# Two up projections of an fp32 transformer block on one Trainium2 core: the high part of the weights times both parts of the activations in one 512-column matmul

## The reference

```python
h = rms_norm(x, ffn_norm_w[layer])
gu = h @ w_gate_up[layer]                      # (256, 1024) @ (1024, 5632)
x = x + (jax.nn.silu(gu[..., :FFN_DIM]) * gu[..., FFN_DIM:]) @ w_down[layer]     # FFN_DIM = 2816
```

## Time and profile before

| what | value |
|---|---|
| median of 3 runs | 1063.54 us (1063.42 to 1064.06) |
| the profiled execution: first to last instruction (span) | 1061.5 us |
| median less span | 2.0 us |
| PE busy | 1045.6 us, 99% |
| DVE busy | 744.9 us, 70% |
| ACT busy | 605.3 us, 57% |
| granted TensorE clock, mean | 1.000 |

### The profile page before, as it was taken

The page is one execution under the profiler, slowest core; times in us unless marked ns, Lnnn a source line. Parts: engine busy times, 40 slices in busy tenths (PEclk is TensorE's granted clock), DMA queues, the critical chain, the costliest instruction groups (busy, mean ns, idle before and its releaser), DMA issues.

```text
span 1061.5 us, 23965 instructions
## 1 busy us (share of the span) xinstructions
PE 1045.6 (99%) x8650; PEld 1009.8 (95%) x8650; DVE 744.9 (70%) x1250; ACT 605.3 (57%) x1100; POOL 152.8 (14%) x160
## 2 busy tenths in 40 slices
PE   8999999999999999999999998999999999999998
PEld 7989999999999889999999998999898999999998
DVE  6875876665555878966655558878867569998743
ACT  7654764445545677654455445665766657666532
POOL 3100021111110000211111110000101034454300
PEclk9999999999999999999999999999999999999999
DMA  8533465555665322555556664444233445555563
GB/s 298 180 134 99 135 227 180 192 179 173 180 188 176 129 100 78 199 196 191 180 178 184 178 194 140 148 151 140 95 126 120 140 159 187 187 179 179 177 199 100
DMA packets 52488, 174.45 MB, mean 164 GB/s; under 512 B 5952, under 2 KB 7232, under 8 KB 52288
## 3 DMA queue, kind: packets, MB, share of 16 engines
q1 hardware_dynamic: 52416, 173.46, 50.0%
HBM read 172.39 MB, written 1.05 MB: 163 GB/s over the span
## 4 chain that ended last, share of the span: by engine, by line
PE 86%; DVE 6%; ACT 3%; issue 1%; DMA 1%; ACTq 0%; SPq 0%; DVEq 0%
PE bank L744 15%; PE bank L745 15%; PE bank L746 15%; PE scores L744 9%; PE scores L745 9%; PE scores L746 9%; DVE ring_lo L1620 2%; PE bank L729 2%; PE bank L730 1%; PE bank L731 1%; PE scores L955 1%; DMA ring_raw<-w_up 1%; ACT ring_hi L1147 1%; DVE tmp L1757 1%; PE bank L873 1%
## 5 line engine op out<-in xcount | busy, mean ns | idle before, releaser
L1620 DVE TENSOR_TENSOR ring_lo<-ring_raw,ring_hi 128x1024 fp32r<-128x1024 f32 (+2 forms) x343 | 399.4, 1167 | 60.3 <-ACT ring_hi L1147 54.5
L1147 ACT ACTIVATE ring_hi<-ring_raw 128x1024 fp32r<-128x1024 f32 (+2 forms) x343 | 341.0, 997 | 71.3 <-PE scores L746 34.0
L744 PE MATMUL bank<-xw_hi,ring_hi 128*128 128x256 f32 x1048 | 302.4, 289 | 1.4 <-DVE ring_lo L1620 0.6
L745 PE MATMUL bank<-xw_lo,ring_hi 128*128 128x256 f32 x1048 | 296.3, 283 | 0.0
L746 PE MATMUL bank<-xw_hi,ring_lo 128*128 128x256 f32 x1048 | 296.2, 283 | 0.0
L744 PEld LDWEIGHTS bank<-xw_hi,ring_hi 128*128 128x128 f32 x1048 | 200.6, 191 | 7.5 <-issue 5.1
L745 PEld LDWEIGHTS bank<-xw_lo,ring_hi 128*128 128x128 f32 x1048 | 200.7, 192 | 0.1
L746 PEld LDWEIGHTS bank<-xw_hi,ring_lo 128*128 128x128 f32 x1048 | 200.6, 191 | 0.0
L744 PE MATMUL scores<-xw_hi,ring_hi 128*128 128x256 f32 x528 | 150.2, 284 | 0.5 <-DVE xw_lo L1626 0.5
L745 PE MATMUL scores<-xw_lo,ring_hi 128*128 128x256 f32 x528 | 149.4, 283 | 0.0
L746 PE MATMUL scores<-xw_hi,ring_lo 128*128 128x256 f32 x528 | 149.4, 283 | 0.0
(11 more groups left out here) (247 smaller groups left out, 1868.5 us busy)
## 6 DMA issues: line engine op xcount, KB each, us to landing
ring_raw<-w_up SPq DMA_DIRECT2D x132, 512.0 KB, 3.2
ring_raw<-w_in SPq DMA_DIRECT2D x85, 512.0 KB, 3.2
ring_raw<-w_down SPq DMA_DIRECT2D x48, 512.0 KB, 3.6
ring_raw<-w_down SPq DMA_DIRECT2D x24, 384.0 KB, 3.9
ring_raw<-w_oa SPq DMA_DIRECT2D x16, 256.0 KB, 2.6
ring_raw<-w_ob SPq DMA_DIRECT2D x16, 256.0 KB, 2.9
ring_raw<-w_oa SPq DMA_DIRECT2D x8, 512.0 KB, 3.2
ring_raw<-w_ob SPq DMA_DIRECT2D x8, 512.0 KB, 3.3
```

The source lines that it names most:

```text
L744: mm(bank[b][:, 0:T], w_hi, tile(hi, t), start=kk == 0, stop=False)
L745: mm(bank[b][:, 0:T], w_hi, tile(lo, t), start=False, stop=False)
L1147: A(ring_hi[:, slot * DM:slot * DM + width], ring_raw[:, slot * DM:slot * DM + width], ACT.Copy).then_inc(hi_done, 1)
L1620: V.tensor_tensor(ring_lo[:, a:b], ring_raw[:, a:b], ring_hi[:, a:b].bitcast(f32), SUB).then_inc(lo_done, 1)
```

## The change

In `up0` and `up1` alone (`HALVES`), high weights by both parts of the activations become one matmul of 512 columns: the low and high parts now lie in one buffer, and the moving operand is a pattern of two pieces of 256 columns. The high weights are loaded once instead of twice. Columns 0 to 255 of the bank then hold high by high plus low weights by high activations, columns 256 to 511 high weights by low activations. The two halves must be added. Since this is done by reading one half from SBUF, ACT first copies the second half of the bank to SBUF (`copy_low`), DVE adds the first half to it, and a second DVE instruction multiplies with `rstd`, in place. Two semaphores are new, `low_copied` and `halves_summed`. All other projections keep their three matmuls; for them only the names of the buffers change.

```diff
+HALVES = ("up0", "up1")
...
+        self.halves = name in HALVES
...
+        low_half = u[:, 0:2 * T]
...
+        def hi_and_lo(parts, a, width=T):
+
+            return parts[:, :].rearrange("p (n c) -> p n c", n=2)[:, :, a:a + width]
...
+            def products(ps, a, parts, t, start, stop, halves=False):
+
+
+                w_hi, w_lo = ring_hi[:, a:a + P], ring_lo[:, a:a + P]
+                x_parts = hi_and_lo(parts, t * T)
+                if halves:
+                    mm(ps[:, 0:2 * T], w_hi, x_parts, start=start, stop=False)
+                else:
+                    mm(ps[:, 0:T], w_hi, x_parts[:, 0, :], start=start, stop=False)
+                    mm(ps[:, 0:T], w_hi, x_parts[:, 1, :], start=False, stop=False)
+                return mm(ps[:, 0:T], w_lo, x_parts[:, 0, :], start=False, stop=stop)
...
-                    mm(bank[b][:, 0:T], w_hi, tile(hi, t), start=kk == 0, stop=False)
-                    mm(bank[b][:, 0:T], w_hi, tile(lo, t), start=False, stop=False)
-                    last = mm(bank[b][:, 0:T], w_lo, tile(hi, t), start=False, stop=end)
+                    last = products(bank[b], a, parts, t, kk == 0, end, ph.halves)
...
+            def copy_low(layer, ph, i, c):
+
+                n = 2 * FT * layer + 4 * i + c
+                act.wait_ge(tile_done, ph.tile(i, c)[1] + 1)
+                if not (type(n) is int and n < 2):
+                    act.wait_ge(halves_summed, n - 1)
+                A(two(low_half, c % 2), bank[ph.bank(i, c)][:, T:2 * T], ACT.Copy).then_inc(low_copied, 1)
+
             def swiglu(layer):
                 def after(ph, i, c):
                     h = c // 2
                     p = FT * layer + 2 * i + h
+                    copy_low(layer, ph, i, c)
                     if c % 2 == 0:
                         act.wait_ge(out_ready, ph.out(i, c) + 1)
                         silu_gate(p, h, two(gate, h))
...
-                    V.tensor_tensor(two(val if c % 2 else gate, h), ps, rstd[:, :], MUL).then_inc(out_ready, 1)
+                    dst = two(val if c % 2 else gate, h)
+                    n = 2 * FT * layer + 4 * i + c
+                    dve.wait_ge(low_copied, n + 1)
+                    V.tensor_tensor(dst, ps, two(low_half, c % 2), ADD).then_inc(halves_summed, 1)
+                    dve.wait_ge(halves_summed, n + 1)
+                    V.tensor_tensor(dst, dst, rstd[:, :], MUL).then_inc(out_ready, 1)
```

More of the change, by code:

```diff
@@ L343, in program @@
         ring_raw = sb("ring_raw", RING * DM)
[L344 to L349, removed]
+        ring_parts = sb("ring_parts", 2 * RING * DM, f32r)
+        act_parts = sb("act_parts", 2 * FT * T, f32r)
+        xw_parts = sb("xw_parts", 2 * KT * T, f32r)
+        ring_hi, ring_lo = ring_parts[:, 0:RING * DM], ring_parts[:, RING * DM:2 * RING * DM]
+        act_hi, act_lo = act_parts[:, 0:FT * T], act_parts[:, FT * T:2 * FT * T]
+        xw_hi, xw_lo = xw_parts[:, 0:KT * T], xw_parts[:, KT * T:2 * KT * T]
         x = sb("x", KT * T)
@@ L433, in program @@
         ffn_hi, ffn_lo = sem("ffn_hi"), sem("ffn_lo")
+        low_copied, halves_summed = sem("low_copied"), sem("halves_summed")
         np_sq, np_ms, np_ln, np_rt, np_nt, np_out = (sem(f"norm_{s}") for s in ("sq", "ms", "ln", "rt", "nt", "out"))
@@ L703, in _, with project @@
             mm = nc.tensor.matmul
-            def project(ph, i, c, hi, lo, ready, halfway=None):
+            def products(ps, a, parts, t, start, stop, halves=False):
[7 more added lines that the diff above has]
+                return mm(ps[:, 0:T], w_lo, x_parts[:, 0, :], start=False, stop=stop)
+            def project(ph, i, c, parts, ready, halfway=None):
                 slot, g = ph.tile(i, c)
@@ L727, in project @@
                             o = bank[b][:, tt * T:(tt + 1) * T]
[L728 to L731, removed]
+                            x_tok = hi_and_lo(parts, t * T + tt * P, P)
+                            mm(o, x_tok[:, 0, :], w_hi, start=not second and k == 0 and tt == 0, stop=False)
+                            mm(o, x_tok[:, 0, :], w_lo, start=False, stop=False)
+                            last = mm(o, x_tok[:, 1, :], w_hi, start=False, stop=second and k == 3 and tt == 1)
                     last.then_inc(tile_done, 1)
@@ L741, in project, with project_first_two @@
                     a = slot * DM + k * P
-                    w_hi, w_lo = ring_hi[:, a:a + P], ring_lo[:, a:a + P]
                     end = part == ph.per - 1 and k == ph.blocks[part] - 1
-                    mm(bank[b][:, 0:T], w_hi, tile(hi, t), start=kk == 0, stop=False)
-                    mm(bank[b][:, 0:T], w_hi, tile(lo, t), start=False, stop=False)
-                    last = mm(bank[b][:, 0:T], w_lo, tile(hi, t), start=False, stop=end)
+                    last = products(bank[b], a, parts, t, kk == 0, end, ph.halves)
                 last.then_inc(tile_done, 1)
-            def project_first_two(ph, hi, lo, ready):
+            def project_first_two(ph, parts, ready):
                 for part in range(2):
@@ L757, in project_first_two @@
                                 ready(t)
[L758 to L762, removed]
+                            last = products(b, c * DM + t * P, parts, t, t == 0, t == KT - 1)
                         if part:
@@ L777, in project_group @@
                             n = ph.out0 + m
-                            b = bank[ph.bank_of[n]][:, 0:T]
+                            b = bank[ph.bank_of[n]]
                             if k0 == 0:
@@ L784, in project_group @@
                                     pe.wait_ge(*mixed(layer, t))
[L785 to L789, removed]
+                                last = products(b, slot * DM + (j * ks + k) * P, act_parts, t, k == 0, k == ks - 1)
                             if k1 == ks:
@@ L813, in root_by_token, with run @@
                 issued["root"] += 1
-            def run(name, hi, lo, ready, q=None, then=None, halfway=None):
+            def run(name, parts, ready, q=None, then=None, halfway=None):
                 ph = PH[name]
                 if name == "kv":
-                    project_first_two(ph, hi, lo, ready)
+                    project_first_two(ph, parts, ready)
                 for c in range(ph.body):
                     if name != "kv" or c >= 2:
-                        project(ph, 0, c, hi, lo, ready, halfway)
+                        project(ph, 0, c, parts, ready, halfway)
                     if name[:2] in ("kv", "in") and c == (3 if name == "kv" else 2):
@@ L829, in run @@
                     for c in range(ph.body):
-                        project(ph, 1, c, hi, lo, ready)
+                        project(ph, 1, c, parts, ready)
                 elif ph.turns > 1:
@@ L833, in run @@
                         for c in range(ph.body):
-                            project(ph, i, c, hi, lo, ready)
+                            project(ph, i, c, parts, ready)
             def stream_ready(q):
@@ L1113, in _ @@
                 mm(bank[6][:, 0:T], tmp[:, 0:P], tmp[:, 0:T], start=True, stop=True)
-            run("kv", act_hi, act_lo, stream_ready(0), 0)
+            run("kv", act_parts, stream_ready(0), 0)
             for layer in range(3):
@@ L1117, in _ @@
                 n_in = PH[f"in{layer}"].n
-                run(f"in{layer}", xw_hi, xw_lo, stream_ready(q), q, follow(layer, 0), amid(layer, 0))
-                run(f"oa{layer}", act_hi, act_lo, mixed_ready(layer), None, follow(layer, n_in), amid(layer, n_in))
+                run(f"in{layer}", xw_parts, stream_ready(q), q, follow(layer, 0), amid(layer, 0))
+                run(f"oa{layer}", act_parts, mixed_ready(layer), None, follow(layer, n_in), amid(layer, n_in))
                 project_group(layer)
-                run(f"up{layer}", xw_hi, xw_lo, stream_ready(q + 1), q + 1)
-                run(f"down{layer}", act_hi, act_lo, ffn_ready(layer))
+                run(f"up{layer}", xw_parts, stream_ready(q + 1), q + 1)
+                run(f"down{layer}", act_parts, ffn_ready(layer))
         @block.scalar
```

## The result

The changed kernel takes 1113.62 us (1112.15 to 1114.25), beside 1063.8 us for the kernel before: a ratio of 1.0465, 95% interval 1.0452 to 1.0478, 49.8 us more. The profiled executions have spans of 1111.5 and 1061.5 us, 50.0 us apart. The forecast was 1118.5 us, within 1100 to 1145.

A forecast was written before the change was run, and what follows sets the result against it. The prediction took a closed ring of ACT and DVE waits, 7.03 us per pair against PE's 5.55, as bound: 27.5 us late per up phase, 55.0 on 1061.5, plus 2.0 outside the span, gives 1118.5 us (range 1100 to 1145).

The forecast's parts named there:

- the ring: Closed path of waits between ACT and DVE in the up0 and up1 loops: 7.03 us per pair; chance 0.82.
- PE's pair: PE's time for a gate and a value tile in the up phases: 5.55 us forecast, 5.76 before.
- hand-offs: Six gaps per pair from an instruction's end to the start of the one waiting for it: 0.53 us in all.
- the one from add to multiply: DVE's multiply waiting for its add, twice per pair: taken as 0.10 us, between rows of 0.04 and 0.15.
- DVE to silu: ACT's silu waiting for DVE's multiply, once per pair: 0.12 us.
- The lower bound: Every hand-off at 0.03 us and the loop as short as written-out code: pair 6.68 us, total 1104.5 us.
- The cover: Weight splits running ahead of PE at the start of an up phase, hiding the first pairs; used up at tile 6.
- tile 47: Tile in down0 whose split follows ACT's table load: forecast ready at 300.6 us, 27.5 us late.
- the table load: ACT's load after the last `ffn_split` of an up phase, before tile 47's split; lateness grows from 25.1 to 27.5 us.
- the forecast 13 ns: PE's gain per contraction block in up0 and up1 from merging two matmuls: 9.4 us over 704 blocks.
- the fall: Rival: stalls in each pair drop PE's clock to 1.2 GHz in the up phases, 1280 us if it stayed low; chance 0.05.
- The dear matmul: Rival: the 512-column matmul's two-piece operand streams at half pace in the up phases, 1206 us; chance 0.03.
- The third rival: PE stays the bound in the up phases and its 9.4 us gain shows: 1054 us; chance 0.08 faster, 0.02 within 0.2%.

The follow-up runs named there:

- order: Changed kernel with ACT's `ffn_split` of a pair moved one step later, behind the copy of the next gate tile: 1057.07 us, ratio 0.9931; once more, 1058.35 us.
- extra_beside: Changed kernel plus one 256-column DVE multiply per pair, behind the even step's split, where DVE stands idle: 1113.16 us, ratio 1.0459.
- extra_on_ring: Changed kernel plus one 256-column DVE multiply per pair, between the odd step's multiply and its split: 1128.48 us, ratio 1.0602.
- pe_only: Changed kernel without ACT's copy and DVE's add, one product left out of both up projections, 512-column matmul kept: 1057.21 us, ratio 0.9925.
- three_mm: Changed kernel with the 512-column matmul taken apart into two of 256 columns; copy, add and multiply kept: 1113.57 us, ratio 1.0456.
- ffn_later: Changed kernel with `ffn_split` moved past ACT's next split only, in front of the next gate tile's copy: 1072.07 us, ratio 1.0064.
- copy_first: Changed kernel with ACT's copy moved in front of the split of its step, `ffn_split` unmoved: 1059.37 us, ratio 0.9949; once more, 1057.95 us.

## Why the prediction was right

**The bound and the ring.** The step that decided, that the queues' fixed order closes a ring longer than PE's pair, was right: the changed kernel waits at each of the edges named, `order` cuts one of them and the loss is gone, and `extra_beside` and `extra_on_ring` separate the ring from the load.

**Its length.** 7.03 us was forecast, 6.83 measured. The two pairs of a loop turn are not alike. In the pair shown above the terms in starts and durations are 0.32, 0.95, 0.36 (for 0.38), 0.42, 0.42, 0.33, 0.94, 0.36, 0.42, 0.34, 1.13, 0.42; five hand-offs are 0.03 or 0.04 us and the one to `ffn_split` is 0.13 (238.34 to 238.47), 0.32 us in all. In the other pair `ffn_split` to split is 0.41, and silu starts 0.13 us behind the multiply (227.46 to 227.59; the timelines of DVE and ACT):

```profile
227.04 0.42 DVE L1755 TENSOR_TENSOR tmp<-tmp,rstd 128x256 f32<-128x256 f32 x1
...
227.59 0.42 ACT L1234 ACTIVATE tmp<-tmp 128x256 f32<-128x256 f32 x1 [1.04 <-DVE tmp L1755]
```

So the hand-offs are 0.37 us in the mean, for the forecast 0.53. The term that was mis-sized is the one from add to multiply, 0.10 us twice where both pairs have 0.04: a value between two rows, for which there was no reason. The 0.12 for DVE to silu came in every other pair of up0. The two copies at 0.36 for 0.38 are most of the rest. The lower bound, with 0.03 for each hand-off, had covered this.

**The cover and the end.** Forecast: tile 47 is 27.5 us late in up0. Measured: PE starts it at 297.23 us, where it started at 273.31 before, 23.9 us late (timeline of the changed kernel; the prediction's 273.13 was worked out from tile 1, and the trace of the kernel before has 273.31):

```profile
290.14 0.39 PE L723 MATMUL bank<-act_parts,ring_parts 128*128 128x256 f32 x1 [0.85 <-DVE ring_parts L1640]
...
297.23 0.39 PE L723 MATMUL scores<-act_parts,ring_parts 128*128 128x256 f32 x1 [1.80 <-DVE ring_parts L1640]
```

Two errors partly cancel here. From the split of tile 4 to DVE's last split of the phase, 21 pairs, it took 143.2 us for the forecast 147.3, 4.1 us less. But the first add started at 144.78 us, not at 144.17, and tile 4's split 0.7 us later than forecast. The stall of 1.80 us behind the table load is the one forecast at 2.3.

In up1 tile 47 is 24.9 us later still, for the forecast 27.5. It is one microsecond more than in up0, and the timelines show where: in up1 silu starts 0.12 us behind the multiply in both pairs of a turn, and every other pair takes 6.93 us (the timelines of DVE and ACT in up1):

```profile
541.17 0.42 DVE L1755 TENSOR_TENSOR tmp<-tmp,rstd 128x256 f32<-128x256 f32 x1
...
541.71 0.42 ACT L1234 ACTIVATE tmp<-tmp 128x256 f32<-128x256 f32 x1 [1.04 <-DVE tmp L1755]
```

Why this hand-off has two lengths stays open. The 1.2 us that are left of the 50.0 come behind tile 47 of up1, and no run looked into them.

**PE.** The block went from 0.360 to 0.347 us, the forecast 13 ns; 0.23 us stand between a 512-column matmul and its neighbour, as forecast. Hidden in the changed kernel, the gain showed in `pe_only` and `order` as 7.9 and 8.1 us. Both are less than the 9 us or more that I had expected.

**The rivals.** The clock was 1.00 in both windows, 136 and 147 us long, with a stall of about 1 us in every pair, so the fall did not come. The Trainium skill's rule on frequent short stalls (TensorE: Matmul & The Clock Gate, section A second HAM failure mode: psum-queue depth-cycling), by which the clock would swing between its levels here, is not borne out at this length of stall. The dear matmul is excluded by `pe_only` and `three_mm`. The third rival, that PE stays the bound, falls with the measured time.

## What to carry to other kernels

A busy share says whether an engine has room, not whether the order of its queue lets it use that room: before moving work to two engines that wait for each other, write out the instructions of one period in order, mark which waits for which, and add up the longest closed path; compare that with the period of the engine that bounds. Here engines at 63% and 48% held the bound, and putting one instruction one step later, with all the work kept, turned 4.7% lost into 0.7% won. What it is worth to merge two matmuls on the engine that bounds is read from the starts: 13 ns a block here, where the record of the matmul that went is 0.28 us long.

## What the hardware showed beyond that

**Two paces of PE at the same clock.** With granted clock 1.00, a block of the up phases (512 + 256 columns) takes 0.347 us or 0.353 us, steady through a phase. `order` in its first execution, starts 0.35 us apart for a block:

```profile
223.86 0.39 PE L721 MATMUL scores<-xw_parts,ring_parts 128*128 128x512 f32 x1
224.09 0.28 PE L725 MATMUL scores<-xw_parts,ring_parts 128*128 128x256 f32 x1
224.21 0.39 PE L721 MATMUL scores<-xw_parts,ring_parts 128*128 128x512 f32 x1
```

`pe_only` in up1 (its up0 had 0.230 us for the first step):

```profile
519.89 0.40 PE L721 MATMUL scores<-xw_parts,ring_parts 128*128 128x512 f32 x1
520.13 0.28 PE L725 MATMUL scores<-xw_parts,ring_parts 128*128 128x256 f32 x1
520.25 0.40 PE L721 MATMUL scores<-xw_parts,ring_parts 128*128 128x512 f32 x1
```

Over the 352 blocks of a phase 7 ns are 2.4 us, about what parts 121.36 from 123.90 in the table. It can also hold the missing 1.5 us of `pe_only`. The stretches of the kernel before, all of 256 columns, had 0.120 in both phases. What draws the pace stays open.

**DVE and GpSimd hold each other up.** In `order`, GpSimd's subtraction falls beside two instructions of DVE, the multiply and the split behind it, each with two inputs in SBUF (timelines of DVE and POOL):

```profile
231.60 0.42 DVE L1756 TENSOR_TENSOR tmp<-tmp,rstd 128x256 f32<-128x256 f32 x1
231.94 1.77 DVE L1641 TENSOR_TENSOR ring_parts<-ring_raw,ring_parts 128x1024 fp32r<-128x1024 f32 x1
...
231.62 1.01 POOL L1570 TENSOR_TENSOR act_parts<-tmp,act_parts 128x256 f32 x1 [4.54 <-ACT act_parts L1229]
```

The split takes 1.77 us for 1.22, the subtraction 1.01 for the 0.74 that it takes in the changed kernel, where it runs beside no instruction of DVE. The Trainium skill (SBUF — State Buffer, section SBUF: two separate sides) has one port pair that the two engines share as an exclusive lock: whichever starts first holds it for its whole instruction, and the other stands. The trace agrees. The multiply started 0.02 us before the subtraction, and the subtraction lost 0.27 us; in up1 the multiply starts 0.08 us before it in every other pair, and the record is 0.94 us long, so that both end about 1.03 us after the multiply's start. The split then started while the subtraction ran, and lost 0.55 us. In `ffn_later` and `copy_first` the subtraction starts before the multiply and keeps its 0.74 us, and the multiply, where it starts 0.55 us after it, takes 0.46 or 0.47 us instead of 0.42. So these engines meet elsewhere than in semaphores too, and in a trace this shows as longer records without idle time. The 0.55 us stand off PE's path here; on the ring they would have cost as much as one and a half short instructions, by an estimate from the 0.34 us of `extra_on_ring`.
